# Three experts instead of two in the weight ring of a hybrid encoder layer, with x2 kept in DRAM meanwhile

## What is computed

```
xn  = rmsnorm(x2, ffn_norm_g)
g   = argmax over 4 groups;  e1, e2 = the two best of that group's 8 experts
y_e = (silu(xn @ w1[e]) * (xn @ w3[e])) @ w2[e]     # w1, w3: 1024 x 512, w2: 512 x 1024
out = rmsnorm(x2 + gate1 * y_e1 + gate2 * y_e2, final_norm_g)
```

## Time and profile before

| what | value |
|---|---|
| median of 3 runs | 1282.28 us |
| the profiled execution: its own time, its span | 1282.33 us, 1280.7 us |
| PE, DVE, ACT, POOL busy | 1127.8, 512.9, 421.2, 256.9 us |
| rawe loads | 96 of 2 MB, issued from 658.7 to 1190.9 us |
| first sigmoid of the expert loop, last | 715.14 us, 1231.76 us |
| weights' waits: cur13a (DVE), all | 29.8 us in 15 places |

### The profile page before, as it was taken

One profiled execution on the slowest core, in us unless ns is written; L12 is line 12 of the kernel. 1 busy time (PEld: TensorE's weight loads), 2 busy tenths in 40 slices (PEclk: granted clock), 3 DMA queues, 4 the chain that ended last, 5 costly groups with the idle time before them and its releaser, 6 DMA issues.

```text
span 1280.7 us, 15752 instructions
## 1 busy us (share of the span) xinstructions
PE 1127.8 (88%) x5184; PEld 692.0 (54%) x5184; DVE 512.9 (40%) x862; ACT 421.2 (33%) x668; POOL 256.9 (20%) x275
## 2 busy tenths in 40 slices
PE   2999999999988977999993899989999889989970
PEld 1788888888856645788883333333333333333320
DVE  3551111111526846755345334433424333434228
ACT  4422222223135645533214124232423333333322
POOL 0011110011106001000000234433434223334220
PEclk9999999999999967999996899989999889989995
DMA  8153331621160000742259699999999999999706
GB/s 294 53 189 107 108 108 69 240 87 49 49 244 11 1 1 9 271 132 102 102 209 424 239 376 390 420 418 418 404 373 357 422 420 419 421 420 399 290 29 277
DMA packets 66735, 299.46 MB, mean 234 GB/s; under 512 B 8816, under 2 KB 8944, under 8 KB 41360
## 3 DMA queue, kind: packets, MB, share of 16 engines
q1 hardware_dynamic: 53632, 264.42, 52.2%
q0 software_dynamic: 13072, 34.63, 7.1%
HBM read 272.28 MB, written 35.91 MB: 241 GB/s over the span
## 4 chain that ended last, share of the span: by engine, by line
PE 61%; DMA 18%; DVE 8%; issue 7%; ACT 5%; SPq 1%; DVEq 1%; ACTq 0%; POOLq 0%; POOL 0%
DMA rawe<-in_w 16%; PE ps L538 12%; PE ps L540 12%; PE ps L539 12%; PE ps L829 12%; PE ps L854 4%; ACT cur L1156 2%; PE ps L637 2%; PE ps L658 1%; PE ps L819 1%; PE ps L670 1%; DVE cur13b L1594 1%; PE ps L755 1%; PE ps L649 1%; DVE att L1315 1%
## 5 line engine op out<-in xcount | busy, mean ns | idle before, releaser
L829 PE MATMUL ps<-cur13a,xT 128*64 128x512 f32 x656 | 163.8, 644 | 36.7 <-DVEq L1596 35.9
L538 PE MATMUL ps<-whi,xTh 128*128 128x512 f32 x480 | 188.5, 393 | 6.2 <-DVE xTl L1252 4.1
L539 PE MATMUL ps<-wlo,xTh 128*128 128x512 f32 x480 | 188.0, 392 | 0.0
L540 PE MATMUL ps<-whi,xTl 128*128 128x512 f32 x480 | 187.8, 391 | 0.0
L1187 DVE TENSOR_TENSOR wlo<-raw,whi 128x2048 fp32r<-128x2048 f32 x27 | 61.7, 2292 | 218.3 <-ACT whi L877 218.0
L829 PE MATMUL ps<-cur13b,xT 128*64 128x512 f32 x656 | 148.5, 592 | 0.0
L1572 DVE COPY xT<-ps 128x512 f32<-128x512 f32 x41 | 28.4, 692 | 296.1 <-PE ps L819 296.1
L854 PE MATMUL ps<-cur,hT 128*64 128x512 f32 x640 | 146.1, 598 | 0.0
L829 PEld LDWEIGHTS ps<-cur13a,xT 128*64 128x64 f32 x656 | 53.2, 147 | 118.3 <-issue 116.1
L928 ACT ACTIVATE zst<-ps 128x512 f32<-128x512 f32 x60 | 35.8, 599 | 235.1 <-PE ps L540 235.1
L1156 ACT ACTIVATE cur<-rawe 128x4096 f32 x31 | 112.3, 3623 | 0.1
(11 more groups left out here) (224 smaller groups left out, 1472.3 us busy)
## 6 DMA issues: line engine op xcount, KB each, us to landing
rawe<-in_w SPq DMA_DIRECT2D x96, 2048.0 KB, 15.9
raw<-in_w_in SPq DMA_DIRECT2D x20, 1024.0 KB, 5.9
z_scratch<-zst POOLq DMA_DIRECT2D x60, 256.0 KB, 2.3
gat<-z_scratch SPq DMA_DIRECT2D x12, 512.0 KB, 3.8
xn_scratch<-rrow POOLq DMA_DIRECT2D x6, 1024.0 KB, 4.7
ya<-y_scratch SPq DMA_DIRECT2D x6, 1024.0 KB, 10.0
raw<-in_w_out SPq DMA_DIRECT2D x4, 1024.0 KB, 6.9
xin<-in_x_prompt SPq DMA_DIRECT2D x4, 512.0 KB, 8.0
```

Source lines behind the costliest of these rows:

```text
L538: pe.matmul(out, ah, bh, start=first, stop=False)
L539: pe.matmul(out, ah, bl, start=False, stop=False)
L540: return pe.matmul(out, al, bh, start=False, stop=last)
L829: mm = pe.matmul(ps[0][u * CAP:(u + 1) * CAP, :], xT[:, c, h * CAP:(h + 1) * CAP], cur13[h][:, :, c * 512 + u * 256:c * 512 + u * 256 + 25 ...
```

## The change

- rawe gets a third slot (RING = 3, slot = expert % 3). It then fills the first 144 KB of each partition, over the projection's whi, wlo, mTh, mTl and over g2. All waits and offsets count by 3; the third slot's semaphores are raised by 16 at the start, so that the counts are of one form. DVE and ACT wait on three slots' semaphores where it was two.
- x2 is held in three row buffers of 4 KB. SyncE writes each tile to x2_scratch in DRAM (`x2_out`) and, behind the last expert's weights, reads all of it back into x2t. DVE waits, from the fourth tile on, until the row buffer is read and stored.
- Expert 0 is issued after the first xres load, behind the wait for the last wlo piece; expert 1 after the last x2_out; experts 2 to 7 after the last rrow; the others in a loop of 2 x 12. gf (the last norm's gain) is loaded behind x2t.
- cur13a moves over the x2 row buffers, the routing tables to F_O under cur13b, xT, xg and ystage behind cur2, hT, sg and hh over the constant `rel` (used by the retention's decay alone). So ACT's first copies wait: cur13a for the last logits, the last rrow and the x2 stores, cur2 for both xn_scratch stores, cur13b for the index table (s_nb), after the routing's two exps.

```diff
+RING = 3
-    x2 = at("x2", D_O + 16 * KB, [P, NT, D])
+    x2 = [at(f"x2{s}", D_O + (32 + 4 * s) * KB, [P, D]) for s in range(3)]
-    g2 = at("g2", D_O + 40 * KB, [P, D])
+    g2 = at("g2", D_O + 16 * KB, [P, D])
-    sel = at("sel", D_O, [P, NT, NE])
+    sel = at("sel", F_O, [P, NT, NE])
...
-    rawe = at("rawe", RAW_O, [P, 2 * EW])
-    cur13 = [at("cur13a", HL_O + 48 * KB, [P, 2, PIECE]), at("cur13b", F_O, [P, 2, PIECE])]
+    rawe = at("rawe", RAW_O, [P, RING * EW])
+    cur13 = [at("cur13a", D_O + 32 * KB, [P, 2, PIECE]), at("cur13b", F_O, [P, 2, PIECE])]
...
+    x2t = at("x2t", 96 * KB, [P, NT, D])
+    gf = at("gf", 120 * KB, [P, D])
...
 # SyncE
+            def expert(p, x, slot=None):
+                held = not isinstance(p, int) or p >= RING
+                slot = p % RING if slot is None else slot
+                if held:
+                    sp.wait_ge(s_c13, 2 * p - (2 * RING - 2))
+                weight(x, slot, 0, s_w1)
+                weight(x, slot, 1, s_w3)
+                if held:
+                    sp.wait_ge(s_cw2, p - (RING - 1))
+                weight(x, slot, 2, s_w2)
+
+            def x2_out(t):
+                sp.dma_start(x2_d[t * P:(t + 1) * P, :], x2[t % 3][:, :]).then_inc(s_x2s[t % 3], 16)
+            for k in (s_w1, s_w3, s_w2):
+                sp.sem_inc(k[2], 16)
             for t in range(NT):
                 if t == 0:
                     sp.wait_ge(s_mgd, 2 * NT)
                 else:
                     sp.wait_ge(s_x2, 2 * t)
+                    x2_out(t - 1)
                 sp.dma_start(xres[:, :], x_tiles[t]).then_inc(s_xr, 16)
-            sp.wait_ge(s_lo, PRE)
-            expert(0, 0)
+                if t == 0:
+                    sp.wait_ge(s_lo, PRE)
+                    expert(0, 0)
+
+            sp.wait_ge(s_x2, 2 * NT)
+            x2_out(NT - 1)
             sp.wait_ge(s_w, 2 * NT)
-            for g in range(1, NG):
-                expert(0, g)
+            expert(1, 8)
+            sp.wait_ge(s_rr, NT)
+            for p in range(2, 8):
+                expert(p, EPG * (p % NG) + p // NG)
+            with sp.Fori(0, 2) as i:
+                for q in range(12):
+                    expert(12 * i + (8 + q), 3 * i + (EPG * (q % NG) + 2 + q // NG), (8 + q) % RING)
+            sp.wait_ge(s_c13, 2 * NE - 4)
+            sp.wait_ge(s_cw2, NE - 2)
+            for s in range(3):
+                sp.wait_ge(s_x2s[s], 32)
+            sp.dma_start(x2t[:, :, :], x2_d.rearrange("(t p) d -> p t d", p=P)).then_inc(s_x2l, 16)
             sp.dma_start(gf[:, :], ...).then_inc(s_gf, 16)
-            with sp.Fori(1, EPG) as j:
-                for g in range(NG):
-                    expert(j, g)
 # ScalarE
-            act.wait_ge(s_w, 2 * NT)
+            def first_up(h):
+                act.activation(cur13[h][:, :, :], ..., ACT.Copy).then_inc(s_c13, 1)
             act.wait_ge(s_w1[0], 16)
             act.wait_ge(s_w3[0], 16)
+            act.wait_ge(s_lg, NT)
+            act.wait_ge(s_rr, NT)
+            for s in range(3):
+                act.wait_ge(s_x2s[s], 32)
+            first_up(0)
             act.wait_ge(s_w2[0], 16)
-            act.wait_ge(s_rst[0], 16 * NT // 2)
+            for s in range(2):
+                act.wait_ge(s_rst[s], 16 * NT // 2)
             act.activation(cur2[:, :], rawe[:, 4 * PIECE:6 * PIECE], ACT.Copy).then_inc(s_cw2, 1)
             act.wait_ge(s_re, 1)
             ...
             act.wait_ge(s_nb, 1)
+            first_up(1)
 # VectorE
+                    if t >= 3 and n == 0:
+                        dve.wait_ge(s_rTm, 2 * (t - 2))
+                        dve.wait_ge(s_x2s[t % 3], 16)
...
                     for k in (s_w1, s_w3):
-                        dve.wait_ge(k[0], 16 * (e1 // 2) + 16)
-                        dve.wait_ge(k[1], 16 * ((e1 + 1) // 2))
-                    pair = rawe[:, bass.ds((e1 % 2) * EW, 4 * PIECE)]...
+                        dve.wait_ge(k[0], 16 * (e1 // 3) + 16)
+                        dve.wait_ge(k[1], 16 * ((e1 + 2) // 3))
+                        dve.wait_ge(k[2], 16 * ((e1 + 1) // 3) + 16)
+                    pair = rawe[:, bass.ds((e1 % RING) * EW, 4 * PIECE)]...
...
+            dve.wait_ge(s_x2l, 16)
```

More of the change, by code:

```diff
@@ L207, in hybrid_layer @@
[L207 to L211, removed]
+    sel = at("sel", F_O, [P, NT, NE])
+    A12 = at("A12", F_O + 768, [P, 2, NT, NE])
+    t1 = at("t1", F_O + 2304, [P, NT, NE])
+    t2 = at("t2", F_O + 5 * KB, [P, 2, NT, NE])
+    Ab = at("Ab", F_O + 3 * KB, [P, NT, NE])
@@ new lines, in hybrid_layer @@
+    wide = at("wide", F_O + 4 * KB, [P, NE])
+    wint = at("wint", F_O + 4 * KB + 128, [P, NE], U32)
+    ends = at("ends", F_O + 4 * KB + 256, [P, NE])
+    zero = at("zero", F_O + 4 * KB + 384, [P, NE])
+    first = at("first", F_O + 4 * KB + 512, [P, NE])
+    last_row = at("last_row", F_O + 4 * KB + 640, [P, NE])
+    bp = at("bp", F_O + 4 * KB + 768, [P, 2, 2, NT], U32)
+    sbf = at("sbf", F_O + 7 * KB, [P, 2, 2, NT])
+    Bt = at("Bt", F_O + 8 * KB, [P, 2 * NT, NB + 1])
+    Rt = at("Rt", F_O + 11 * KB, [P, NT, P])
@@ L227, in hybrid_layer @@
-    yo = [at(f"yo{t}", HL_O + (1 + t) * 4 * KB, [P, D]) for t in range(NT)]
-    fj = [at(f"fj{s}", HL_O + (7 + s) * 4 * KB, [P, D]) for s in range(2)]
+    x2t = at("x2t", 96 * KB, [P, NT, D])
+    gf = at("gf", 120 * KB, [P, D])
+    yo = [at(f"yo{t}", HL_O + t * 4 * KB, [P, D]) for t in range(NT)]
+    fj = [at(f"fj{s}", HL_O + (6 + s) * 4 * KB, [P, D]) for s in range(2)]
     ps = [ctx.enter_context(nc.psum_tensor(f"ps{i}", [P, 512], F32)) for i in range(8)]
@@ L308, in hybrid_layer @@
         s_x2 = sem("s_x2")
+        s_x2s = [sem(f"s_x2s{s}") for s in range(3)]
+        s_x2l = sem("s_x2l")
         s_rp = sem("s_rp")
@@ L328, in hybrid_layer @@
         s_sgm = sem("s_sgm")
-        s_w1 = [sem(f"s_w1{s}") for s in range(2)]
-        s_w3 = [sem(f"s_w3{s}") for s in range(2)]
-        s_w2 = [sem(f"s_w2{s}") for s in range(2)]
+        s_w1 = [sem(f"s_w1{s}") for s in range(RING)]
+        s_w3 = [sem(f"s_w3{s}") for s in range(RING)]
+        s_w2 = [sem(f"s_w2{s}") for s in range(RING)]
         s_c13 = sem("s_c13")
@@ L491, in _, with weight @@
             sp.dma_start(gcol[:, :], A["ffn_norm_g"][0].rearrange("(p c) -> p c", c=KC)).then_inc(s_rp, 16)
+            def weight(x, slot, k, done):
+                c = slot * EW + k * 2 * PIECE
+                sp.dma_start(rawe[:, c:c + 2 * PIECE].rearrange("p (h n) -> p h n", h=2),
+                             e_w[k][bass.ds(x, 1)][0]).then_inc(done[slot], 16)
+            def expert(p, x, slot=None):
[12 more added lines that the diff above has]
+                sp.sem_inc(k[2], 16)
             for t in range(NT):
@@ L852, in down @@
                             c = h * PIECE + k * D + u * 512
-                            w2 = rawe[:, EW + 4 * PIECE + c:EW + 4 * PIECE + c + 512] if last else cur2[:, c:c + 512]
+                            w2 = rawe[:, LAST_W2 + c:LAST_W2 + c + 512] if last else cur2[:, c:c + 512]
                             mm = pe.matmul(ps[6][u * CAP:(u + 1) * CAP, :], hT[:, k, h * CAP:(h + 1) * CAP],
@@ L1152, in step @@
                 with act.If(e > e0):
[L1154 to L1156 removed]
+                    act.wait_ge(s_w2[0], 16 * (e // 3) + 16)
+                    act.wait_ge(s_w2[1], 16 * ((e + 2) // 3))
+                    act.wait_ge(s_w2[2], 16 * ((e + 1) // 3) + 16)
+                    act.activation(cur2[:, :], rawe[:, bass.ds((e % RING) * EW + 4 * PIECE, 2 * PIECE)],
                                    ACT.Copy).then_inc(s_cw2, 1)
@@ L1169, in _ @@
                     act.wait_ge(s_sq3, t - 1)
-                act.activation(fj[t % 2][:, :], x2[:, t, :], ACT.Square, accum_out=ssq[:, t:t + 1]).then_inc(s_sq3, 1)
+                act.activation(fj[t % 2][:, :], x2t[:, t, :], ACT.Square, accum_out=ssq[:, t:t + 1]).then_inc(s_sq3, 1)
         @block.vector
@@ L1500, in _ @@
                     dve.wait_ge(s_rp, 16 * 4)
-                dve.scalar_tensor_tensor(out=rrow[t % 2][:, :], in0=x2[:, t, :], scalar=rstd[:, t:t + 1],
+                dve.scalar_tensor_tensor(out=rrow[t % 2][:, :], in0=x2[t % 3][:, :], scalar=rstd[:, t:t + 1],
                                          in1=g2[:, :], op0=ALU.mult, op1=ALU.mult).then_inc(s_rr, 1)
```

75 lines of the change are left out of this document (27 added, 48 removed).

## The result

The changed kernel takes 1270.85 us (median of 7 runs, 1269.63 to 1277.61), the kernel before beside it 1283.27: ratio 0.991, 95% interval 0.9895 to 0.9925. Faster, but by 12 us where 23 were forecast, and outside the forecast's range by 2. The profiled execution took 1270.85 us itself, its span 1268.8.

The account below looks back on a forecast made before the run. Neither engine alone bound the loop: some blocks were set by the weights, others by their own work, with 36.2 us lost to late weights. 1282.33 less 23.2 (last sigmoid earlier) gave 1259.1 us, range 1250 to 1269.

Parts of the forecast that it names:

- the early expert 0: Before the loop: three 2 MB pieces queued ahead of the second xres make the start 1.5 us later, bounds 0 and +4.
- the arrival of expert 26: In the expert loop: its weights land at 1099.2 instead of 1121.73, at 16.04 us an expert; blocks wait 3.4 us.
- the first sigmoid was after 719: Start of the expert loop: sign that the prediction is wrong; it expected the first sigmoid near 716.6.
- the x2 write: Before the loop: x2 tiles stored to DRAM, six writes of 0.5 MB, costed at 0.
- the routing tables' new home: Before the first block: ACT's first copies wait for logits, stores and index table; cost 0, +2 us at most.
- anchor: Start of the stream count: ACT's copy of expert 3 into cur2, ending at 773.6 before, shifted by 1.5 and 0.5 us.
- The stall behind expert 14: In the weight stream: 8.6 us lost while expert 14's three blocks keep both slots full; goes, 0 to 2 may stay.
- The margin of 2 us: At w2 of expert 18: expert 15's copy into cur2 ends near 968, the stream asks near 970.
- Register work: DVE ahead of its copy: a third value and two more waits, 0.15 us per new-expert block, bounds 0 and 0.3.
- Reading x2 back: Behind the last w2, near 1185: 3 MB and gf in 8 us, first used over 30 us on; cost 0.
- Rival D: In the loop: gathers land late behind the deeper queue, each block losing 2.3 us; 1351 us, chance 5%.
- Rival C: Weight stream slower, 16.3 us an expert (5 us at expert 26), or its stall stays (8.6); 1264 to 1273, chance 15%.

Follow-up runs that it names:

- light_w2: Changed kernel with expert 0 issued last, DVE's register waits ahead of the multiplies, and half of each w2 left out from expert 3 on (layer not computed): 1241.35 us.
- hold2: Changed kernel, but SyncE waits as for two slots, so one of the three stays empty: 1292.51 us (one run).
- late0: Changed kernel, but expert 0 is issued after the last xres load, where it was before; three slots stay: 1266.1 us, ratio 0.9864.
- spread0: Changed kernel, but w1, w3 and w2 of expert 0 are issued one by one behind the xres loads of row tiles 1, 2 and 3: 1266.28 us.
- waits_ahead: Changed kernel, but DVE's six register waits stand between its copy to xT and the two multiplies: 1270.14 us, ratio 0.9895.
- two_regs: Kernel before, two slots, with two more long-satisfied register waits at a value divided by 3 ahead of the copy into cur13a: 1287.3 us, ratio 1.0033.
- late0_waits_ahead: Changed kernel with expert 0 issued last and DVE's register waits ahead of the multiplies: 1263.57 us, ratio 0.9837.
- x2_thrice: Changed kernel, but x2 is read back three times, one after the other, and DVE waits for the third: 1269.83 us, ratio 0.9894.
- two_early0: Kernel before, two slots, with only expert 0 issued early, behind the first xres load and the last wlo wait: 1288.51 us, ratio 1.0033.

## Why the prediction was wrong, step by step

The mechanism was right: neither engine bound the loop alone, the third slot put the stream ahead, and experts 26 and 30 bind at the end (light_w2, hold2). The sum was 11.8 us short. Two of its terms failed, the early expert 0 and the arrival of expert 26; with either of them right the time would have stood at some 1267 to 1268 (1270.85 less 3.8, or less 3.2, see below), inside the range. One of the prediction's own signs came: it called itself wrong if the first sigmoid was after 719. By its own terms (which add up to 1259.2):

| term | forecast | profile after | missed |
|---|---|---|---|
| first sigmoid | 716.6 | 722.32 | 5.7 |
| first sigmoid to expert 26's copy | 382.6 | 387.12 | 4.5 |
| that copy to the last sigmoid | 109.4 | 110.39 | 1.0 |
| last sigmoid to the end of the execution | 50.6 | 51.0 | 0.4 |

**Expert 0 loaded earlier: +1.5 us, bounds 0 and +4, was 5.3.** This is the first step that failed. The second xres was to land at 614.6 and landed at 618.4. Windows of the changed kernel (columns as the earlier trace rows):
```profile
595.00:596.00 1.00, 1.00 (x6) 0.83 (x5) 0.52 (x1) 0.00 (x0) 0.00 (x0) 1.00 0.30 66
596.00:597.00 1.00, 1.00 (x6) 0.84 (x5) 0.00 (x0) 0.00 (x0) 0.00 (x0) 1.00 0.85 360
...
617.00:618.00 1.00, 0.00 (x0) 0.00 (x0) 0.00 (x0) 0.00 (x0) 0.00 (x0) 1.00 0.06 25
```
Of the 3.8 us, 0.8 is the execution's own. The weights, issued at 593.7, moved at full rate only from 596, which is 2.3 us and not 1.5. From there the three pieces, the x2 write and xres beside the store took until about 617, 21 us and not 19.5. The add came 1.4 us later and not 0.7. Then PE, which the sum had late by 1.5 us, stood still for 3.67, and its clock fell for part of the next stretch, which the sum had not counted: that is the other 1.6. The changed kernel, then late0:
```profile
601.00:618.00 17.00, 14.60 (x81) 12.43 (x79) 3.99 (x12) 3.14 (x6) 0.70 (x1) 1.00 0.91 361
618.00:626.00 8.00, 6.73 (x23) 5.48 (x24) 5.44 (x15) 2.12 (x4) 0.69 (x1) 0.79 0.43 155
```
```profile
601.00:618.00 17.00, 17.00 (x93) 14.60 (x93) 6.43 (x22) 5.33 (x10) 0.70 (x1) 1.00 0.43 157
618.00:626.00 8.00, 8.00 (x48) 6.95 (x46) 3.84 (x8) 1.09 (x2) 0.69 (x1) 1.00 0.49 195
```
The prediction had the price of every load in the queue, but with no margin on any of them, and its upper bound left out what a stall of PE costs in clock, though its own row of 6.05 us had shown that. The Trainium skill (DMA: Bandwidth & Descriptors, the section on queues, rings and completion order) says that each DMA engine takes the descriptors of a ring in order. The trace agrees: an xres landed 17.1 us after its issue behind three weight pieces, and 3.8 to 4.5 in late0, without them.

The last 1.0 us before the first sigmoid lies behind the last x2 add (44.9 us, 43.9 before). It is no price of the routing tables' new home: late0 and spread0 have the same moves and take 43.8 and 43.9. 0.6 of it is DVE's wait for the last logits from PE, 2.77 us instead of 2.13; why PE is later there stays open.

**The arrival of expert 26: no stall and 16.04 us an expert, was 4.1 us later by the same anchor.** This is the second step that failed. The stall behind expert 14 was to be "0 to 2". The rate over 956 to 986 in the changed kernel, and in waits_ahead:
```profile
956.00:986.00 30.00, 28.23 (x132) 10.94 (x132) 16.36 (x15) 7.70 (x13) 10.31 (x11) 1.00 0.91 364
```
```profile
956.00:986.00 30.00, 29.80 (x138) 11.40 (x139) 17.86 (x15) 12.63 (x13) 15.74 (x11) 1.00 1.01 418
```
Against 420 GB/s that is 30 x (1 - 306 / 420) = 8.1 us lost before, 4.0 after, 0.1 with shorter blocks. In the changed kernel it lies in two places: near 961 to 966, where w1 and w3 of expert 18 are issued at 963.2, behind DVE's copies of expert 15; and near 976 to 979, where w2 is issued at 977.1, behind ACT's copy, which ended at 977.03. The margin of 2 us was counted for the second alone, and blocks 0.19 us longer than counted used it up by expert 15.

But waits_ahead, without the stall, has expert 26 landed only 1.4 us sooner by the anchor (the end of expert 3's copy into cur2): 1101.48 - 775.21 = 326.3 us, against 1109.44 - 781.71 = 327.7. So 2.6 of the 4 us came back as a slower stream. The forecast had 323.6 there. What the two queues moved in these stretches, packets, MB, share of the engines' time, in the changed kernel and in waits_ahead (q1 is SyncE's, q0 POOL's):
```profile
q1 hardware_dynamic: 16459, 126.96, 93.5%
q0 software_dynamic: 4240, 8.31, 6.7%
```
```profile
q1 hardware_dynamic: 16583, 127.93, 94.5%
q0 software_dynamic: 4240, 8.31, 6.7%
```
Gathers and scatters are the same 8.31 MB, so it isn't that shorter blocks put more of them beside the weights. The 60 pieces up to w3 of expert 26 are 125.8 MB. What is above that was moved for pieces behind them: 1.1 MB in one, 2.1 in the other, and the 1.0 between is 2.5 us of SyncE's rate. So the queue was as fast, but more of what it moved wasn't yet wanted. That the break behind expert 14 is what keeps this low in the changed kernel fits these rows and wasn't tested. From expert 26 to 30 the stream took (1174.41 - 1109.44) / 4 = 16.24 us an expert. The kernel before has 16.24 there too (1186.67 - 1121.73, over 4), a row that the prediction passed over.

**Register work: 0.15 us, was 0.34** (12.37 less 12.03), beyond its upper bound of 0.3. The trace has a group more and two waits, as counted, but the idle ahead of the copy grew from 0.25 to 0.50, and the copy itself reads 2.39 instead of 2.29. That the two waits and the value are the cause is shown by two_regs. Its price in time was near the forecast's 1 to 3 us: 1.1 in waits_ahead, 2.9 in late0_waits_ahead, 3.9 in two_regs. It also overlaps with the late weights: without any wait expert 26's copy would have begun at 1109.44 - 3.73 + 0.50 = 1106.21, 383.9 us after the first sigmoid, so 1.3 of the 4.5 us would be there with the weights as forecast, and they alone added 3.2.

**What held.** The anchor: the copy of expert 3 into cur2 ends 59.4 us after the first sigmoid, forecast 59.0, and the experts follow one further on. The routing tables' new home costs nothing that shows (late0). Reading x2 back is hidden (x2_thrice); the x2 write wasn't quite, for with it ahead the second xres kept DVE waiting for 12.0 us and without it for 10.2 (two_early0). Rival D, late gathers: the trace has one wait for a gather, that of the first block, 8.0 us against 8.1 before. The prediction gave D no ground if a gather never waits for the depth of SyncE's queue. hold2 shows that it does, by 3.8 us at the first gather; in the loop the gathers had the cover for it. Rival C was nearest: its stall and its slower stream both came, in part. That the time lies within its 1264 to 1273 owes as much to the late start, which is none of C's.

## What to carry to other kernels

A load moved earlier on a queue is paid by the small loads behind it: count every byte ahead of the next transfer that something waits for, and when the sum is close, split the large load between the small ones (spread0) or put it last. A deeper ring is worth its lead plus the stalls that it bridges, and no more once the stream itself is the end. Then work taken from the blocks is won only until the next expert that is late. Where a margin of 2 us decides over a stall of 9, a term of 0.2 us that recurs 14 times is part of that margin.

## What the runs showed of the hardware

- Two waits on computed counts and one value more made a block 0.34 us longer, with two slots as with three. The group that computes the value takes 0.11 us of that, so a wait is worth some 0.11 (an estimate: what is left, by two). Moved ahead of DVE's multiplies all of them vanish (pitch 11.85, 0.12 above a block without a copy), but late weights then hold the multiplies, 0.8 us each time.
- A late load can cost more than its lateness, through PE's half clock, and the same wait can cost it or not. PE's first 16 multiplications of expert 26, in the changed kernel and in spread0:
```profile
1111.93 6.29 PE L850 MATMUL ps<-cur13a,xT 128*64 128x512 f32 x16 [3.72 <-DVEq L1631]
```
```profile
1106.90 3.65 PE L851 MATMUL ps<-cur13a,xT 128*64 128x512 f32 x16 [3.70 <-DVEq L1632]
```
  In late0 a wait of 1.99 us was enough (15.47 us for the step, 12.37 without a wait), and one of 1.72 in the changed kernel wasn't (13.50).
- A gather on POOL's queue was in use 6.7 us after its issue with SyncE's queue full of weights, and 2.9 us after it with that queue empty (changed kernel, hold2).
